# Pooling weights and bias: loaded once between the loops and scaled there by GpSimd

## What is computed

```python
def pool_mixer(x, w, b, scale):
    ...
    pooled = jnp.concatenate(means, axis=-1) - xf
    y = jnp.einsum('bsgc,gcd->bsgd', pooled.reshape(B, S, N_POOL_GROUPS, POOL_GROUP_DIM),
                   w.astype(jnp.float32)).reshape(B, S, D) + b.astype(jnp.float32)
    return (y * scale.astype(jnp.float32)).astype(x.dtype)
```

## Time and profile before

| | |
|---|---|
| median of 3 runs | 2070.35 us (2069.07 to 2072.57) |
| time of the profiled execution | 2071.23 us |
| its span, first to last instruction | 2069.4 us |
| mean granted TensorE clock | 0.952 of full speed |
| PE busy | 1811.6 us, 88% of the span |
| DVE busy | 822.7 us, 40% |
| ACT busy | 385.7 us, 19% |
| POOL busy | 127.3 us, 6% |
| memory read, written | 577.90 MB, 8.39 MB |

### The profile page before, as it was taken

One profiled execution on the slowest core, in us unless ns is written; L12 is line 12 of the kernel. 1 busy time (PEld: TensorE's weight loads), 2 busy tenths in 40 slices (PEclk: granted clock), 3 DMA queues, 4 the chain that ended last, 5 costly groups with the idle time before them and its releaser, 6 DMA issues.

```text
span 2069.4 us, 34718 instructions
## 1 busy us (share of the span) xinstructions
PE 1811.6 (88%) x14742; PEld 1154.3 (56%) x14742; DVE 822.7 (40%) x1340; ACT 385.7 (19%) x889; POOL 127.3 (6%) x186
## 2 busy tenths in 40 slices
PE   8998776777799877767769999999999999999998
PEld 4756455455557645545554448746554448746553
DVE  5651111111144111111114753474656763473656
ACT  3511011011012101101112112222122122222221
POOL 1200000000000000000000501200211001200000
PEclk9999988988899988889889999999999999999999
DMA  8699999999999999999998675443546374443331
GB/s 335 182 365 412 420 421 420 420 420 420 419 397 381 420 420 420 420 420 420 420 420 328 168 223 174 137 148 137 173 152 203 110 232 165 136 160 124 132 122 61
DMA packets 182134, 592.79 MB, mean 286 GB/s; under 512 B 51156, under 2 KB 52564, under 8 KB 132952
## 3 DMA queue, kind: packets, MB, share of 16 engines
q1 hardware_dynamic: 173432, 571.65, 70.8%
q0 software_dynamic: 8544, 18.89, 3.6%
HBM read 577.90 MB, written 8.39 MB: 283 GB/s over the span
## 4 chain that ended last, share of the span: by engine, by line
PE 57%; DMA 17%; SPq 15%; DVE 6%; issue 2%; ACT 1%; DVEq 0%; ACTq 0%
PE ps L652 18%; DMA ring<-in_moe_w_dram 17%; PE ps L619 9%; SPq L1398 8%; PE ps L1678 5%; SPq L1407 5%; PE ps L1713 3%; PE ps L1658 3%; PE ps L625 3%; SPq L507 3%; PE ps L596 1%; PE ps L1969 1%; PE ps L629 1%; PE ps L534 1%; PE ps L1733 1%
## 5 line engine op out<-in xcount | busy, mean ns | idle before, releaser
L1678 PE MATMUL ps<-ring,xT 128*32 128x128 f32 x8192 | 307.8, 310 | 175.3 <-DMA ring<-in_moe_w_dram 170.1
L1678 PEld LDWEIGHTS ps<-ring,xT 128*32 128x32 f32 x8192 | 266.5, 122 | 242.9 <-DMA ring<-in_moe_w_dram 185.5
L2395 DVE TENSOR_TENSOR arena<-arena,ps 128x256 f32<-128x256 f32 x32 | 13.5, 421 | 558.3 <-ACT arena L2063 558.3
L619 PE MATMUL ps<-xT,ring 128*128 128x256 f32 x896 | 200.9, 383 | 2.6 <-DMA ring<-in_w_in_dram 2.6
L652 PE MATMUL ps<-ring,xT 128*128 128x512 f32 x432 | 194.2, 594 | 0.5 <-ACT xT L786 0.5
L1093 DVE TENSOR_TENSOR ring<-ring 128x2048 f32<-128x2048 f32 x80 | 183.4, 2292 | 19.8 <-PE ps L652 5.7
L619 PEld LDWEIGHTS ps<-xT,ring 128*128 128x128 f32 x896 | 169.2, 191 | 28.9 <-DMA ring<-in_w_in_dram 3.4
L1713 PE MATMUL ps<-arena 128*32 128x512 f32 x768 | 119.9, 606 | 31.6 <-DVE arena L2395 31.6
L1331 POOL DMA_DIRECT2D ring<-gap_bias x160 | 96.0, 618 | 788.7 <-DMA ring<-in_w_in_dram 475.6
L1658 PE MATMUL ps<-arena,x_tm 128*128 128x128 f32 x1024 | 134.8, 287 | 0.0
L1658 PEld LDWEIGHTS ps<-arena,x_tm 128*128 128x128 f32 x1024 | 126.3, 201 | 10.4 <-issue 10.3
(11 more groups left out here) (316 smaller groups left out, 2025.9 us busy)
## 6 DMA issues: line engine op xcount, KB each, us to landing
ring<-in_moe_w_dram SPq DMA_DIRECT2D x287, 1024.0 KB, 26.0
ring<-in_w_in_dram SPq DMA_DIRECT2D x52, 2048.0 KB, 9.2
arena<-in_moe_w_dram SPq DMA_DIRECT2D x89, 1024.0 KB, 26.8
ring<-in_w_br_diff_dram SPq DMA_DIRECT2D x4, 2048.0 KB, 10.3
ring<-in_w_out_dram SPq DMA_DIRECT2D x4, 2048.0 KB, 8.0
arena<-in_moe_w_dram SPq DMA_DIRECT2D x14, 512.0 KB, 15.9
ring<-in_w_mem_kv_dram SPq DMA_DIRECT2D x3, 2048.0 KB, 18.3
ring<-in_mla_w_o_dram SPq DMA_DIRECT2D x1, 4096.0 KB, 27.1
```

The source lines that it names most:

```text
L619: m = nc.tensor.matmul(bank[:, u * T:(u + 1) * T], w[:, k, f * P:(f + 1) * P], xT[:, k, :], start=(k == 0), stop=(k == KD - 1))
L1678: m = nc.tensor.matmul(ps[SL * q:SL * q + SL, g % 2, s * P:(s + 1) * P], xs[:, g % 2, k, s * SL:(s + 1) * SL], w[:, c0:c0 + 2 * P - 1:2], ...
```

## The change

The early loads, GpSimd's products and the writes at the start are taken out, with the two buffers in memory and VectorE's wait for the writes. Between the loops SyncE now loads `pool_scale` (into `pscale`, the second half of down slot 0), `pool_b` and `pool_w` from the inputs, the last two into their final places. GpSimd waits in `scale_pool` for the three, multiplies `pb` and then `pw` in place, and adds to `pool_scaled`; TensorE (L2007) and VectorE (L2563) wait for both products in place of the loads. The input's weights lie as `g (k p) n`, so that each partition takes 8 pieces of 1 KB; `pw_dram` gave it one piece of 8 KB.

```diff
@@ -289,7 +289,7 @@
         pool_places = places(pool_slot, 0, UPW, (KD, PG), (len(WINDOWS) * TT * T,)) + [carve(vec_slot, 0, D)]
-        pw_raw, pb_raw, psc_raw = carve(arena, 0, KD, PG), carve(arena, 6 * D, D), carve(arena, 8448, D)
+        pscale = carve(vec_slot, D, D)
         pool_gain, pool_shift = places(gain_slot, 0, DNW, (D,), (D,))
@@ -377,8 +377,6 @@
         gap_bias = nc.dram_tensor("gap_bias", (BIASES, RUN, GAPS), F32).ap()
-        pw_dram = nc.dram_tensor("pw_dram", (P, KD * PG), F32).ap()
-        pb_dram = nc.dram_tensor("pb_dram", (P, D), F32).ap()
         memT_dram = nc.dram_tensor("memT_dram", (P, KD * T), F32).ap()
@@ -1507,10 +1505,6 @@
             load_route(sp, 1)
-            sp.wait_ge(sem("qT_ps"), 8)
-            for dst_, src_ in ((psc_raw, a["pool_scale"]), (pb_raw, a["pool_b"])):
-                sp.dma_start(dst_, src_[0].partition_broadcast(P)).then_inc(sem("pool_in"), 16)
-            sp.dma_start(pw_raw, a["pool_w"][0].rearrange("g (k p) n -> p g k n", p=P)).then_inc(sem("pool_in"), 16)
             sp.wait_ge(sem("o_ps"), NH)
@@ -1547,9 +1541,10 @@
             load_mem_w(sp, 1, 0)
-            sp.wait_ge(sem("gap_pool_out"), 48)
-            sp.dma_start(pb, pb_dram).then_inc(sem("pool_in"), 16)
-            sp.dma_start(pw, pw_dram.rearrange("p (k n) -> p k n", k=KD)).then_inc(sem("pool_in"), 16)
+            for dst_, src_ in ((pscale, a["pool_scale"]), (pb, a["pool_b"])):
+                sp.dma_start(dst_, src_[0].partition_broadcast(P)).then_inc(sem("pool_in"), 16)
+            sp.dma_start(pw.rearrange("p (g k) n -> p g k n", k=2),
+                         a["pool_w"][0].rearrange("g (k p) n -> p g k n", p=P)).then_inc(sem("pool_in"), 16)
             sp.dma_start(pband, a["band"]).then_inc(sem("band_g_in"), 16)
@@ -2004,7 +1999,7 @@
                     if t == n == 0:
-                        pe.wait_ge(sem("pool_in"), 80)
+                        pe.wait_ge(sem("pool_scaled"), 2)
                     for u in range(2):
@@ -2288,8 +2283,6 @@
                 begin_root(v)
-                if n == 0 and t:
-                    v.wait_ge(sem("gap_pool_out"), 48)
                 if n == 3 and t:
@@ -2560,7 +2553,7 @@
             pw, pband, pb = pool_places
-            v.wait_ge(sem("pool_in"), 80)
+            v.wait_ge(sem("pool_scaled"), 2)
             for t in range(TT):
@@ -2571,6 +2564,15 @@
             dve_second(v)
+
+        def scale_pool(pool):
+
+            pw, _, pb = pool_places
+            pool.wait_ge(sem("pool_in"), 48)
+            nc.gpsimd.tensor_tensor(pb, pb, pscale, ALU.mult).then_inc(sem("pool_scaled"), 1)
+            by_group = pw.rearrange("p (g k) n -> p g k n", k=2)
+            nc.gpsimd.tensor_tensor(by_group, by_group, over(pscale.rearrange("p (g n) -> p g n", n=PG), 2, 2),
+                                    ALU.mult).then_inc(sem("pool_scaled"), 1)
@@ -2583,18 +2585,9 @@
             pool.dma_start(gap_bias, over(bias_mask[0:BIASES, :], 1, RUN)).then_inc(sem("gap_pool_out"), 16)
-
-            pool.wait_ge(sem("pool_in"), 48)
-            pool.wait_ge(sem("o_ps"), NH)
-            by_group = pw_raw.rearrange("p (g k) n -> p g k n", k=2)
-            nc.gpsimd.tensor_tensor(by_group, by_group, over(psc_raw.rearrange("p (g n) -> p g n", n=PG), 2, 2),
-                                    ALU.mult).then_inc(sem("pool_scaled"), 1)
-            nc.gpsimd.tensor_tensor(pb_raw, pb_raw, psc_raw, ALU.mult).then_inc(sem("pool_scaled"), 1)
-            pool.wait_ge(sem("pool_scaled"), 2)
-            pool.dma_start(pw_dram.rearrange("p (k n) -> p k n", k=KD), pw_raw).then_inc(sem("gap_pool_out"), 16)
-            pool.dma_start(pb_dram, pb_raw).then_inc(sem("gap_pool_out"), 16)
-
             for layer in range(DEPTH):
+                if layer:
+                    scale_pool(pool)
                 pool.wait_ge(sem("mkv_taken"), 4 * layer + 2)
@@ -2602,7 +2595,7 @@
             pool.wait_ge(sem("loops_done"), 1)
-            pool.wait_ge(sem("gap_pool_out"), 48)
+            pool.wait_ge(sem("gap_pool_out"), 16)
             pool.wait_ge(sem("mk_out"), 16 * DEPTH)
...
```

## The result

| | before | after |
|---|---|---|
| median of 20 runs | 2070.56 us (2065.30 to 2073.34) | 2073.40 us (2071.79 to 2074.61) |
| ratio, 95% interval | | 1.0013 [1.0007, 1.0019] |
| profiled execution: time, span | 2071.23, 2069.4 us | 2074.5, 2072.7 us |
| mean granted TensorE clock | 0.952 | 0.955 |
| memory read, written | 577.90, 8.39 MB | 576.33, 6.82 MB |

The changed kernel is 2.8 us slower (1.4 to 3.9 by the interval): the interval lies clear of 1, and the loss is 0.14%. The page says that it reads and writes 1.57 MB less each and that VectorE's share of the chain is a little up, 7% against 6%. The shares of PE, DMA and SPq moved by more, but their sum is 90% against 89%: they only changed places, and say little.

What follows compares the result with a forecast made beforehand. Expert loops were taken as DMA-limited, the stretches between as a TensorE and VectorE chain. Start 0, lock 3.7 and clock 1.55 gave +5.25 us: 2075.6 against the median, own range 2074 to 2077.5, whole range 2069.5 to 2078.5.

Steps and rivals of the forecast that it cites:

- The lock: Between the loops, GpSimd's two products exclude VectorE's two-input norm steps; TensorE gets x_tm 3.7 us late (3.2 to 4.4).
- the walk: Turn-by-turn timing between the loops: pb's product holds L2264, pw's holds L2265, and L2305 ends at 622.2, not 618.53.
- Rival B: GpSimd's products miss the norm between the loops (tiny steps exempt or pw after 614.1): 0 to +1 us, 2070.9; chance 0.24.
- The clock: Behind TensorE's idle hole between the loops, the granted clock falls: +1.55 us, bounds 0 to 3.45.
- the row with the like hole: First loop, L1713: after 2.91 us idle, 32 matmuls took 5.19 us against 3.64, pricing the slow clock at 1.55.
- The arrivals: Loads between the loops: extra 0.5 MB and 1 KB rows make pw land at 612.4 (611.7 to 614.4), band at 614.9.
- Rival D: Between the loops pw lands at 620 or after; TensorE waits 4.9 us, clock adds 1.55; time 2077.2, chance 0.07.
- Does it reach the end: Second loop starts and ends later by what the chain lost; the added DMA time of 1.25 + 0.65 us vanishes.
- The sum: Whole kernel: 0 + 3.7 + 1.55 = +5.25 us, forecast 2075.6 against the median.
- taken out at the start: Removing the start's three loads, two GpSimd products and two writes was valued at 0, bounds 0 to -3.7 us.
- rival C: Removed writes relieve a DMA backlog in the first loop, 3.7 us less; later stretch +0.5; time 2067.2, chance 0.05.
- Rival A: Between the loops TensorE idles 3.7 us but keeps its clock rate; time 2074.1, chance 0.08.

Runs made afterwards that it cites:

- scalar_root: Changed kernel with the norm's three one-element two-input VectorE steps written as tensor_scalar; ratio to the kernel before 1.0011 [1.0002, 1.0020], stretch 55.4 us.

## Why the prediction was right or wrong

**The lock: right, in mechanism and size.** Two tiny steps held, for 2.13 and 4.44 us; the walk had 2.29 and 4.5. TensorE got x_tm at 621.28. The timeline of TensorE in the kernel before:

```profile
608.00 7.07 PE L1604 MATMUL ps<-ring 128*128 128x256 f32 x32
614.90 7.07 PE L1998 MATMUL ps<-ring,x_tm 128*128 128x256 f32 x32
```

Its second half of L1998 starts 3.45 us in, at 618.35, and the changed kernel ran 0.70 us ahead (L1599 at 607.30 against 608.00): 621.28 - 617.65 = 3.6 us late, with 3.7 forecast. Three runs show that it is the meeting and not the products: later products (53.6), products on another engine (52.5), one more product (62.2). Rival B is out: tiny steps are held, though not in every form.

**The clock: right in the changed kernel, for a reason that is not complete.** 5.41 - 3.72 = 1.69 us, 1.55 forecast from the row with the like hole. But in scalar_root and the two kernels with the start kept, holes of 2.24, 2.45 and 3.16 us left the 16 matmuls at 3.72. In the three profiles where the clock fell (holes of 2.40, 2.44 and 6.64 us), a short wait of 0.80, 0.62 and 0.60 us for the band matrix came 3.7 us ahead of the long one; in those where it did not, the band was in time. This goes with it six times out of six, and was forecast once, for the second run of the start kept; no run put the short wait in or took it out alone. A rival fits as well: the hole comes at another moment in each execution, and no run separates this from the short wait. So the cause of the fall is open, and that the changed kernel showed it in both of its profiles, as forecast, is in part luck.

**The arrivals: right.** pw at 612.6 (612.4 forecast), the band at 615.1 (614.9). The forecast had the band just in time, and it was late as TensorE came 0.70 us earlier; the 0.80 us is hidden behind x_tm, which is later still. Rival D is out.

**Does it reach the end: right.** Loop 1 took 459.5 to 460.3 us in 13 of the 14 profiles (462.0 in the other), at starts from 654.8 to 663.5 us. A late start is not made up.

**The sum: the stretch came out at 5.4 and 5.3 us with 5.25 forecast, the whole kernel at 2.8 (1.4 to 3.9).** So the terms are right where they were placed, and the whole got about 2.5 us less. The forecast's own range, 2074 to 2077.5, was missed by 0.6 us: the 2073.4 measured lies inside the whole range that took in the rivals. And the chance of 0.53 stood on a loss of over 0.2%, where the loss was 0.14%. Two steps are candidates, and both are in the last table.

The first is the work "taken out at the start", "Value: 0". Against kernels that keep it, its removal is worth about 2.3 us, within the bound of -3.7 kept for a backlog. But the kernel that keeps it and has VectorE's products does all the work of the kernel before in a stretch of 52.7 us and is still 1.9 us slower (0.0 to 3.5), so the new loads seem to cost nearly as much, a term that the prediction let vanish; this is argued from the ratios, and no profile shows where. The two together come to -0.4 us in VectorE's kernel, twice: each of the two zeros was probably wrong, and that their sum is nearly right is luck. A part of this lies outside the span. In the three runs without a product of GpSimd on the pooling weights (VectorE's, twice, and the products left out) 2.18 to 2.29 us of each execution lie around the span, in all others 1.73 to 1.86. No run says why. Within the span VectorE's kernel is thus 0.8 us faster than the kernel before, and the removal worth 2.7. The forecast's argument rested on the DMA share at 140 to 145 us, and that window is dry (0.32 to 0.82) in every profile, with the work and without it. Nor do the profiles show the worth in the first loop, where rival C had it: that loop takes 457.7 us in the mean of the five profiles with the work at the start and 457.7 in the mean of the nine without. What does differ is the load before it. Windows of the kernels with VectorE's products, first with the start kept, then without:

```profile
120.00:135.00 15.00, 15.00 (x65) 8.88 (x64) 7.93 (x20) 3.03 (x5) 0.53 (x1) 1.00 1.01 419
```

```profile
120.00:135.00 15.00, 15.00 (x66) 8.99 (x65) 6.96 (x17) 3.03 (x5) 0.57 (x1) 1.00 0.80 301
```

The second is "the clock after the hole", 1.55 us, taken as paid in each execution. The three kernels whose profile has the fall are 2.2 to 3.0 us better than their stretch says, and the six others without the work at the start -0.9 to +0.8. If most timed executions kept the clock, as the one profile of the tiny-step kernel did behind a like hole, 1.7 us of the missing 2.5 are there, and with the 0.8 us from above 5.3 - 1.7 - 0.8 = 2.8, as measured, though each of these terms is uncertain by 1 to 2 us. It isn't shown: each run has one profile, and the mean granted clock of an execution (about 0.955 for both kernels) doesn't tell, as most of what it lacks is lost inside the expert loops (0.88 of full speed from 200 to 600 us in the kernel before, 0.90 in the changed one). Rival A, the lock without the clock, gives 2074.1, nearer to the 2073.4 measured than the forecast's 2075.6, though both profiled executions of the changed kernel show the fall.

**What stays open** is which executions have the fall, and where the removal's us come back and the new loads' are lost. The stages around the change vary too much by themselves: the first loop took 456.5 us in one profile of the kernel before and 458.4 in the other, so the 2.0 us that it was shorter in the changed kernel are no evidence. Of the 1.8 us behind the loops 1.7 have a place, the first projection matmuls behind a wait for weights. In the kernel before:

```profile
1232.54 8.86 PE L619 MATMUL ps<-xT,ring 128*128 128x256 f32 x32 [2.00 <-DMA ring<-in_w_in_dram]
```

In the changed kernel:

```profile
1237.47 7.17 PE L617 MATMUL ps<-xT,ring 128*128 128x256 f32 x32 [2.19 <-DMA ring<-in_w_in_dram]
```

The group ran slow in both profiles of the kernel before and in that of the wait for the norm, and in none of the six whose TensorE had the hole between the loops; 14 profiles are too few to call that an effect. If it is one, it is a third way in which the whole gets less than the stretch. Rival C had the sign of the start's term right, but the new loads take it back.

None of these versions beats the kernel before by more than can be told. The best keeps the change and gives the products to VectorE: 0.9998 twice, with 1.57 MB less written and read back, and 2.7 to 3.1 us faster than the change as it was made.

## What to carry to other kernels

Before work goes to an idle engine, look at what its neighbour does at that moment: at the start GpSimd's products held no VectorE step, and here they delayed TensorE by 3.6 us, since a norm lay beside them with 2.9 us of slack. In the kernel before they ran from 94.94 to 101.74 us, and VectorE's next instruction was this:

```profile
101.85 0.69 DVE L2282 SCALAR_TENSOR_TENSOR x_tm<-x_tm,ps 128x512 f32<-128x512 f32 x1 [10.19 <-PE ps L1969]
```

A lock is counted in turns: each GpSimd product can hold one two-input step of VectorE, however small, for as long as the product still runs (1.2 to 4.3 us here), and the slack must cover the sum. When an owner of the critical data has idle time of its own behind its last urgent step (4.81 us here), it is the better place for small work, even if the other engine is empty.

## What the runs showed of the hardware that was not expected

- A `tensor_scalar` whose second operand is a value per partition in SBUF takes 0.21 us under a running GpSimd product; a `tensor_tensor` on the same one-element tiles is held for up to 4.44 us.
- A GpSimd product's record includes its own wait for a turn: 5.49 us in scalar_root, where VectorE's held L2297 went in between, against 4.50.
- The same product of 128x2048 takes 4.50 us on GpSimd and 2.29 on VectorE; of 128x1024, 2.34 and 1.22.
- The granted clock does not follow the length of the last hole alone: 1.00 behind 3.16 us, 0.67 behind 2.40 us with a wait of 0.80 us shortly before.
- Two profiles of one kernel differ by up to 2 us in a loop limited by DMA, while the stretch between the loops repeats to 0.7 us.
- The time of an execution outside its span was 2.18 to 2.29 us in every execution of the three runs without a GpSimd product on the pooling weights, and 1.73 to 1.86 us in all others.
